# Seven products per pair of tiles in the first network, and the modulation groups moved into its first phase

## What is computed

```
mod = silu(cond) @ w_mod + b_mod            # 1024 x 9216, two conditioning vectors
sh0, sc0, g0, sh1, sc1, g1, sh2, sc2, g2 = split(mod, 9)
h = rms_norm(x, n_pre[0]) * (1 + sc0) + sh0
x = x + 0.5 * g0 * rms_norm(swiglu(h, f_in[0], f_out[0]), n_post[0])      # first network
h = rms_norm(x, n_pre[1]) * (1 + sc1) + sh1
x = x + g1 * rms_norm(token_mixer(h), n_post[1])                          # mLSTM and attention
h = rms_norm(x, n_pre[2]) * (1 + sc2) + sh2
x = x + 0.5 * g2 * rms_norm(swiglu(h, f_in[1], f_out[1]), n_post[2])      # second network
swiglu(h, w_in, w_out) = (silu(h @ w_in[:, :2816]) * (h @ w_in[:, 2816:])) @ w_out
```

## Time and profile before

| | |
|---|---|
| time, median of 3 runs | 1715.86 us (1715.79 to 1718.55) |
| the profiled execution's own time | 1714.82 us |
| its span, first to last instruction | 1713.0 us |
| TensorE busy | 1692.3 us, 99% of the span |
| DVE, ACT busy | 1016.9 us (59%), 693.4 us (40%) |
| granted TensorE clock | 1.00 |
| moved from and to memory | 189.50 MB, mean 111 GB/s |

### The profile page before, as it was taken

The page is one execution under the profiler, slowest core; times in us unless marked ns, Lnnn a source line. Parts: engine busy times, 40 slices in busy tenths (PEclk is TensorE's granted clock), DMA queues, the critical chain, the costliest instruction groups (busy, mean ns, idle before and its releaser), DMA issues.

```text
span 1713.0 us, 27947 instructions
## 1 busy us (share of the span) xinstructions
PE 1692.3 (99%) x11327; PEld 1561.3 (91%) x11327; DVE 1016.9 (59%) x1723; ACT 693.4 (40%) x1272; POOL 0.2 (0%) x4
## 2 busy tenths in 40 slices
PE   8999999999999999999999999999999999999998
PEld 6999899989979989999999888889889988998997
DVE  5756465666465323555537877774646834772775
ACT  6322222212364332343445655553464433551452
POOL 0000000000000000000000000000000000000000
PEclk9999999999999999999999999999999999999999
DMA  9535343433214224323333211111621221332233
GB/s 388 175 135 220 136 159 135 157 139 123 90 59 158 75 64 105 100 81 82 100 135 97 98 53 41 42 41 50 220 77 62 80 92 62 95 94 83 73 103 146
DMA packets 58650, 189.50 MB, mean 111 GB/s; under 512 B 7672, under 2 KB 16680, under 8 KB 56744
## 3 DMA queue, kind: packets, MB, share of 16 engines
q1 hardware_dynamic: 58536, 187.89, 33.1%
HBM read 170.67 MB, written 16.54 MB: 109 GB/s over the span
## 4 chain that ended last, share of the span: by engine, by line
PE 89%; DVE 4%; ACT 3%; issue 1%; DMA 1%; DVEq 0%; ACTq 0%; SPq 0%
PE psum L711 13%; PE psum L713 12%; PE psum L712 12%; PE psum L814 4%; PE psum L816 4%; PE psum L815 4%; PE psum L693 4%; PE psum L695 4%; PE psum L694 4%; PE psum L1235 2%; PE psum L1217 2%; PE psum L783 2%; PE psum L785 2%; PE psum L784 2%; PE psum L1195 2%; PE psum L1120 1%
## 5 line engine op out<-in xcount | busy, mean ns | idle before, releaser
L1868 DVE TENSOR_TENSOR wlo<-raw,whi 128x1024 fp32r<-128x1024 f32 x148 | 181.2, 1224 | 370.9 <-ACT whi L1329 370.8
L1329 ACT CAST whi<-raw 128x1024 fp32r<-128x1024 f32 x148 | 154.7, 1045 | 327.8 <-PE psum L816 141.7
L711 PE MATMUL psum<-h_hi,whi 128*128 128x320 f32 x720 | 223.8, 311 | 0.0
L713 PE MATMUL psum<-h_hi,wlo 128*128 128x320 f32 x720 | 222.5, 309 | 0.0
L712 PE MATMUL psum<-h_lo,whi 128*128 128x320 f32 x720 | 222.4, 309 | 0.0
L711 PE MATMUL psum<-g_hi,whi 128*128 128x320 f32 x656 | 209.4, 319 | 0.2 <-ACT gate L1686 0.2
L713 PE MATMUL psum<-g_hi,wlo 128*128 128x320 f32 x656 | 202.7, 309 | 0.0
L712 PE MATMUL psum<-g_lo,whi 128*128 128x320 f32 x656 | 202.6, 309 | 0.0
L711 PEld LDWEIGHTS psum<-h_hi,whi 128*128 128x128 f32 x720 | 135.1, 188 | 4.6 <-issue 4.5
L712 PEld LDWEIGHTS psum<-h_lo,whi 128*128 128x128 f32 x720 | 135.2, 188 | 0.0
L713 PEld LDWEIGHTS psum<-h_hi,wlo 128*128 128x128 f32 x720 | 135.1, 188 | 0.0
(11 more groups left out here) (440 smaller groups left out, 3700.6 us busy)
## 6 DMA issues: line engine op xcount, KB each, us to landing
raw<-in_w_ffn_in SPq DMA_DIRECT2D x88, 512.0 KB, 3.6
raw<-in_w_mix SPq DMA_DIRECT2D x77, 512.0 KB, 4.1
raw<-in_w_ffn_out SPq DMA_DIRECT2D x44, 512.0 KB, 3.5
mw<-in_w_mod SPq DMA_DIRECT2D x28, 768.0 KB, 5.1
mw<-in_w_mod SPq DMA_DIRECT2D x8, 1024.0 KB, 16.7
gate<-gate_keep SPq DMA_DIRECT2D x24, 320.0 KB, 5.0
mw<-in_w_mod SPq DMA_DIRECT2D x14, 512.0 KB, 4.5
gate_keep<-gate SPq DMA_DIRECT2D x20, 320.0 KB, 4.6
```

Of the source, the lines that this page charges most:

```text
L711: mm(out, wh[:, k, :], hi[:, k, cols], start=(k == 0), stop=False)
L713: last = mm(out, wl[:, k, :], hi[:, k, cols], start=False, stop=(k == nk - 1))
L1329: copy((to or whi[t.slot])[:, :, :], raw[t.raw][:, :, :]).then_inc(w_hi, 1)
L1868: tt(lo[:, :, :], raw[t.raw][:, :, :], hi[:, :, :].bitcast(F32), ALU.subtract).then_inc(raw_free, 1)
```

## The change

1. **First network, phases two and three**: all 14 pairs (8 and 6) go by `seven`. The token sums for them are made while TensorE works on phase one's output tiles. `h_lo` takes the place of `h2_lo`; the fourth weight sum lies where `rb` is; other PSUM banks are used (`pair_banks`, `OUT_BANKS`).
2. **Modulation**: all 14 groups are finished within phase one and its first output tiles. Groups 0 to 6 stay on DVE, with two `macc` buffers, 2 to 4 chunks per tile (`STEPS`). Groups 7 to 13 don't pass DVE: SP loads each as one transfer of 2 MB into one of two buffers (`direct`, in the space of `x` and of `y`), and `sum_direct` makes it on TensorE with 16 matmuls of 256 columns. `DIRECT_AFTER` and `SUM_AFTER` say behind which tile. Turning the rows moves from phase three into phase two's output tiles.
3. **Border of the first network**: its output weights are split late, as in the second network (`row_weights`: tile 0 in `whi`/`wlo`, 1 to 4 in `rows_w`), not ahead into the modulation's space; the order of its rows (`row_order`) stays. The residual `x_tok` is loaded at the end of phase three in two parts and no longer in phase one.
4. The loops over tiles in the first network are written out.

```diff
+SEVEN = {(0, 1): range(8), (0, 2): range(6), (1, 0): range(4, 8), (1, 1): range(8), (1, 2): range(6)}
+ON_VECTOR = 7
+STEPS = (4, 3, 4, 3, 3, 3) * 2 + (3, 3, 2)
+SUM_AFTER = {3: 0, 6: 1, 9: 2, 11: 3, 14: 4, 16: 5, 18: 6}
+DIRECT_AFTER = {5: 0, 6: 1, 8: 2, 10: 3, 12: 4, 14: 5, 16: 6}
+DIRECT_LOAD = {12: 2, 13: 3, 15: 4, 17: 5, 19: 6}
...
+        macc = [at(f"macc{s}", [P, 2, MOD_W], F32, at_ + KC * MOD_W * 4) for s, at_ in enumerate((mw_at, x_at))]
+        direct = [at(f"direct{s}", [P, KC, MOD_W], F32, at_) for s, at_ in enumerate((x_at, r1))]
...
         def row_weights(l, u, base):
-            if l == 2:
+            if l != 1:
                 if u == 0:
                     return whi[(base + 1) % 2], wlo[(base + 1) % 2]
...
+            def load_direct(m):
+                if m >= 2:
+                    sp.wait_ge(direct_done, m - 1)
+                sp.dma_start(direct[m % 2][:, :, :].rearrange("p k c -> p (k c)"),
+                             a["w_mod"][ON_VECTOR + m]).then_inc(direct_in[m % 2], 16)
...
+                for c in range(10, T_MIX):
+                    for q in steps_at(c - 6) if c < 22 else ():
+                        n, k = divmod(q, KC)
+                        for part in range(3):
+                            if k == MOD_K[part][1] - 1 and n + 1 < ON_VECTOR:
+                                load_mod(n + 1, part)
+                    load_tile(c)
+                    if c in DIRECT_LOAD:
+                        load_direct(DIRECT_LOAD[c])
...
+                    if c == T_MIX - 3:
+                        sp.wait_ge(prod_done, KEEP + 5 * (FIRST_PAIRS[2] - 1) + 4)
+                        load_tokens(slice(0, 2))
+                load_tokens(slice(2, NT))
...
+            def sum_direct(m):
+                pe.wait_ge(direct_in[m % 2], 16 * (m // 2 + 1))
+                for k in range(KC):
+                    at_ = (k + 1) * MOD_COLS - 2 * (ON_VECTOR + m)
+                    for half in range(2):
+                        last = mm(mod_part(2 * (k % 2) + half, half), silc_pad[:, at_:at_ + MOD_COLS],
+                                  direct[m % 2][:, k, half * MOD_HALF:(half + 1) * MOD_HALF], start=False, stop=False)
+                last.then_inc(direct_done, 1)
...
+                        for c in range(3, 2 * nj):
+                            project(Tile(c), KC, h_hi, h_lo)
+                            sums_after(c)
...
+                    for n in SEVEN.get((f, p), ()):
+                        seven(SEVEN_FROM[f, p] + n, n, base)
...
+                            if f == 0 and p == 0:
+                                if v in (2, 3, 4):
+                                    top_sums(*((0, 1), (1, 4), (4, 5))[v - 2], 0)
+                                if v in (4, 5):
+                                    token_sums(*((0, 2), (2, 5))[v - 4], 0)
+                                if v >= KC - 2:
+                                    for j in ((1, 0), (2, 3))[v - KC + 2]:
+                                        token_low(j, 0)
```

More of the change, by code:

```diff
@@ L97, with steps_at @@
 V_PRE, V_POST, V_MN, V_CC, V_QG, V_KG, V_N = 72, 96, 120, 128, 144, 145, 146
+def steps_at(c):
+    first = KC + sum(STEPS[:c - 4])
+    return range(first, first + STEPS[c - 4])
 def row_order(l):
@@ L226, in build @@
         rows_w = [[[at(f"row_w{l}_{u}_{n}", [P, KC, P], F32R, row_home(l, u)[n]) for n in range(2)]
-                   for u in range(nu)] for l, nu in enumerate((3, 5, 4))]
-        first_w = [[at(f"first_w{u}_{n}", [P, KC, P], F32R, others[0] + (2 * u + n) * whole) for n in range(2)]
-                   for u in range(2)]
+                   for u in range(nu)] for l, nu in enumerate((4, 5, 4))]
+        first_w = [at(f"first_w{n}", [P, KC, P], F32R, (blocks[0], others[0])[n] + 4 * whole) for n in range(2)]
         part = KH * HALF * 4
@@ L520, in ffn, with load_tokens @@
+            def load_tokens(rows):
+                tokens = a["x_tok"].rearrange("p (c d) -> p c d", c=NT)
+                sp.dma_start(x_tok[:, rows, :], tokens[:, rows, :]).then_inc(x_back, 16)
+            def ffn(base):
                 j0 = 0
                 for p, nj in enumerate(PHASES):
[L523 to L527, removed]
@@ L908, in ffn @@
             def ffn(f, base):
[L909 removed]
+                j0 = 0
                 for p, nj in enumerate(PHASES):
[L911 to L952 removed]
@@ L1954, in seven, with token_sums @@
                     pair_low(n, s)
-            def token_sums(first, last):
+            def token_sums(first, last, f):
+                h_lo_ = stages[2 * f][1]
                 def of_h(h, ks, cols):
@@ L2327, in ffn @@
-                    it += nj // 2
+                                token_low(u, 1)
+                    if f == 1 and p == 0:
+                        tiles_in(0, peeled=True)
+                        tiles_in(4, entry=True)
+                    elif p == 0:
+                        for past in range(0, 2 * nj, 4):
+                            tiles_in(past, start=(past == 0))
+                    pairs = SEVEN.get((f, p), ())
+                    for n in pairs:
+                        seven(SEVEN_FROM[f, p] + n, n, base, pairs.start, n == pairs.stop - 1, p == 2, NJ * f + j0)
```

545 lines of the change are left out of this document (254 added, 291 removed).

## The result

| | kernel before | changed kernel |
|---|---|---|
| median of its runs | 1715.82 us (4 runs, 1715.3 to 1718.55) | 1704.98 us (4 runs, 1702.62 to 1706.45) |
| profiled execution, its span | 1714.82, 1713.0 us | 1704.33, 1702.6 us |
| mean granted clock in it | 1.000 | 0.997 |

Ratio 0.9932, 95% interval 0.9915 to 0.9950, which is 11.7 us; the medians alone differ by 10.8 us (ratio 0.9937), where 14.1 were forecast (1701.7). The time lies in the range given (1697.4 to 1709.0).

What follows compares the result with a forecast made beforehand. TensorE, busy 1692.3 of 1713.0 us, was taken as the bound. Terms -24.6 - 5.3 + 14.3 - 0.6 + 1.5 + 0.5 = -14.2 us gave 1700.6 on the profiled execution, 1701.7 us on the median; range 1697.4 to 1709.

Steps and rivals of the forecast that it cites:

- Terms 1 and 2: First network on TensorE: 14 pairs at 12.32 instead of 14.08 us, -24.6 us; 7 of 14 sums dropped, -5.3 us.
- Term 3: Phase one on TensorE: seven direct groups of 16 matmuls add 14.3 us; three saved changeovers give back 0.6 us.
- Term 5: Entry into seven products: DVE's 14 token operations fit within phase one's output tiles; +0.5 us, bounds 0 and 3.
- At nothing: DVE's added work in phase one, turning the rows and the residual's load would cost no time; DVE busy 76 of 100 us.
- Rival A: Phase one: transfers bind, 35.7 MB in 129 us is too much; kernel slower, 1722 us; chance 0.04.
- rival B: Phase one: DVE or a group's load late, 0.5 us behind each of seven groups, 3.5 us, so 1705; chance 0.12.
- Term 4: First network's border: late-split output weights stall row 0 by 1.9 us and delay DVE's chain; +1.5 us, bounds 0 and 5.
- rival C: First border: mixer's first tiles land behind the residual, costing 5 us; with a late entry (3 us), 1707.7; chance 0.12.
- The two delays overlap: First border: row 0's 1.9 us stall and DVE's later taking of row 0 overlap, so +1.5 us was taken.

Runs made afterwards that it cites:

- dummy matmuls: Changed kernel with three dummy matmuls filling TensorE's wait for the fourth output tile in the first border: 1705.51 us, ratio 0.9939.
- order by halves: Changed kernel with the first border's rows 0 and 1 taken in alternating halves, as in the last border: 1704.47 us, ratio 0.9934.
- the residual's move: Changed kernel with only the load of the residual's rows 2 to 4 (1.5 MB) put behind the mixer's first four weight tiles: 1701.69 us, ratio 0.9923.
- the fourth tile early: On top of the residual's move, the border's fourth output tile is cast and subtracted ahead of the last pair's parts: 1701.6 us, ratio 0.9909.
- both edits: Changed kernel with the residual's move and the row order by halves together: 1701.25 us, ratio 0.9915.
- transfers in another order: On top of the fourth tile early, both residual parts load behind the mixer's first two tiles; row 0's last two tiles go in sequence: 1703.96 us, ratio 0.9924.

## Why the prediction was right, and where it was off

- **Terms 1 and 2, pairs and sums (-24.6, -5.3): right.** Pairs of 12.32 us, in the first network as in the second.
- **Term 3, direct groups (+14.3, -0.6): right.** 1.86 us each to the next line; the profile of the experiment without them gave 13.4 back. The low bound (only streaming, 1.72 a group) and the high one (2.38) are excluded by these rows. That the four column groups work side by side, read from eight matmuls at the start, carried this term.
- **Term 5, the entry (+0.5): right**, 0.38 us of waiting, and 99.16 - 98.56 = 0.6 us in all. With these the border's start was met: 449.14, forecast 464.78 - 15.7 = 449.1.
- **At nothing, DVE and transfers in phase one: right.** DVE 74 of 100 us (forecast 76), and 14 us more would have been free. Rival A did not come: direct loads of 2 MB landed after a median of 9.4 us, and no wait on `direct` or `raw` stands in the profile. Nor did rival B: there is none on `macc` or `wlo`. One remark under rival A is not shown, that the 10.9 us of the 2.5 MB load are mostly latency and tail: at the 422 GB/s of the earlier trace rows its bytes alone would take 6.2. That more traffic would have bound was not tried.
- **Term 4, the border (+1.5, bounds 0 to 5): the mechanism right, the size off.** Measured +4.4. Its first half was met: 1.9 us on row_w forecast, 1.77 measured. What failed is one term of "it must split two tiles of the mixer, whose load ... takes 4.1, so about 12.3 us after the start": DVE took row 0 after 464.43 - 449.14 = 15.3 us. SP asked for the second of these tiles when forecast, 6.02 us after the start (5.95), but it took 7.0 us until ACT could cast it, not 4.1; the cast and the subtraction behind it took what the sum gave them:

```profile
455.16 0.33 SPq L501 DMA_DIRECT2D raw<-in_w_mix  x1
```

  I took the landing time of a weight tile from the median of all of them, though 1.5 MB of residual stood ahead in the same queue, which I had named, as upper bound. With the residual moved the same tile was asked for at 454.71 and cast at 458.30, 3.6 us later. These 2.9 to 3.0 us (15.3 - 12.3 for DVE) are what the term is off (4.4 - 1.5). This is rival C's mechanism, to which I had given 0.12. "The two delays overlap" was right, though both waits show: row 0 made 0.8 us shorter (dummy matmuls) lengthened the wait on `y` by 0.85, and without its stall (order by halves) the border was no shorter.
- **What no term had: the granted clock.** The prediction took 1.00 from the windows of before and held it fixed. The stall in row 0 brought 3.4 us of half clock, which lengthened row 0 by 1.4 to 1.6 us but lay under the late `y`; the gates, which the change doesn't touch, had another 3.4 behind them (1.6 lost in full). The sum of what was missed, 4.4 - 1.5 in the border and 1.6 at the gates, less 0.8 in the mixer's border, is 3.7 us: the difference between 14.2 and 10.5 us on the profiled executions. The 1.6 at the gates compare two single executions. The kernel before has lower clocks too: of its 32 executions beside the experiments 11 had a mean clock of 0.997 or 0.998. So it is not shown that the change makes the half clock more frequent there.
- **The mixer's border, 0.8 us shorter**, was not forecast. The kernel before waits 0.25 us for `row_w` there (at 1225.06) and the changed one doesn't; the rest is not explained.

The three lowest medians of complete versions all have the residual's move: alone (1701.69 us, 0.9923), with the row order by halves (1701.25, 0.9915) and with the fourth tile early (1701.6, 0.9909). They are 3.3 to 3.7 us below the changed kernel's 1704.98, and 1.5 to 4 us by the ratios. Each interval by itself overlaps the changed kernel's, so the gain is likely and its size open; against each other they are not told apart.

## What to carry to other kernels

Where one engine is busy 99% of the span, its own rows price the removed and added matmuls to a few tenths of a microsecond in all, even in a form seen only once; the error sits at the stage borders. There, price a load by what stands ahead of it in its queue, not by its median landing time, and follow the chain behind it for two more rows: of six repairs tried on this border, only the move of a load removed a wait without putting another in its place. A short stall on TensorE can lengthen its stretch by more than its own length, since the clock may fall behind it; whether that reaches the end depends on whether another chain is later still.

## What the runs showed of the hardware

- The granted clock fell to 0.5 (1.2 GHz) behind a wait of TensorE of only 1.77 us, and, in ten of twelve profiles, behind 3.1 us of tiny matmuls and transposes with no wait at all. A stretch lasted 3.4 or 6.8 us and lengthened its place by 1.4 to 1.6 us per 3.4. It didn't follow always: not behind the 1.77 us in two of six profiles, nor behind a wait of 3.3 us (both edits) and one of 2.5 us (transfers in another order). The Trainium skill ("TensorE: Matmul & The Clock Gate", Part 1) has the clock set by how busy TensorE has been recently. The waits agree with that. The tiny matmuls agree only if the profile's busy time is not what counts, since that calls the engine busy for 3.2 of 3.2 us there.
- Part of the spread between executions goes with this clock: the changed kernel took 1702.62 us at a mean clock of 0.999 and 1706.45 at 0.996. Of 32 executions of the kernel before, those at 1.000 took 1714.87 to 1716.48 us and those at 0.997 took 1718.12 to 1718.58; at 0.999 they spread from 1713.92 to 1717.38, so the clock isn't all of it.
- 32 records of a 256-column matmul on four column groups took 1.93 us; the same 16 matmuls over the full width would have been 16 x 0.52 = 8.3 us by the earlier trace rows.
